# Eight rows of every down projection as seven-product groups, and the convolution's taps placed after a PSUM copy

## The reference

```python
def swiglu(x, w_gate, w_up, w_down):              # D_FF = 2816, two in each of two layers
    return (jax.nn.silu(x @ w_gate) * (x @ w_up)) @ w_down
...
up = h @ w_up[l]                                  # D_FF_2 = 3072, once, in the third layer
gate_h = causal_dwconv(up[..., :D_FF_2], ffn_conv_w[l], ffn_conv_b[l])   # three taps over positions
hid = jax.nn.gelu(gate_h) * up[..., D_FF_2:]
x = x + rms_norm(hid @ w_down[l], g_ffn_post[l])
```

## Time and profile before

| | us |
|---|---|
| median of 3 runs | 2766.65 |
| the three runs | 2766.55 to 2767.83 |
| the profiled execution: its own time | 2767.5 |
| its span, first to last instruction | 2765.7 |

### The profile page before, as it was taken

One profiled execution on the slowest core, in us unless ns is written; L12 is line 12 of the kernel. 1 busy time (PEld: TensorE's weight loads), 2 busy tenths in 40 slices (PEclk: granted clock), 3 DMA queues, 4 the chain that ended last, 5 costly groups with the idle time before them and its releaser, 6 DMA issues.

```text
span 2765.7 us, 43073 instructions
## 1 busy us (share of the span) xinstructions
PE 2752.3 (100%) x17466; PEld 2456.1 (89%) x17466; DVE 1844.3 (67%) x2529; ACT 1496.5 (54%) x2334; POOL 117.1 (4%) x130
## 2 busy tenths in 40 slices
PE   9999999999999999999999999999999999999999
PEld 8998887599998899998976799988987889999888
DVE  7766466767773587773667587753876746888638
ACT  6554343565563585553536565543755536666435
POOL 0000000000000000000000000000001100000000
PEclk9999999999999999999999999999999999999999
DMA  7773324037752237753241257733233223776331
GB/s 216 176 184 111 114 58 97 18 104 192 187 142 99 89 91 203 177 143 100 77 101 41 90 141 183 180 100 107 77 98 91 90 85 106 186 183 151 122 115 61
DMA packets 146965, 337.79 MB, mean 122 GB/s; under 512 B 34256, under 2 KB 58192, under 8 KB 146768
## 3 DMA queue, kind: packets, MB, share of 16 engines
q1 hardware_dynamic: 133376, 286.79, 33.4%
q0 software_dynamic: 13248, 48.24, 10.4%
q10 hardware_dynamic: 144, 0.00, 0.0%
HBM read 330.79 MB, written 2.10 MB: 120 GB/s over the span
## 4 chain that ended last, share of the span: by engine, by line
PE 94%; DVE 4%; ACT 1%; issue 1%; DMA 0%; SPq 0%; DVEq 0%; ACTq 0%
PE banks L676 29%; PE banks L677 29%; PE banks L678 29%; DVE WL L551 1%; PE banks L1178 1%; PE banks L1200 1%; ACT WH L546 1%; PE banks L1237 1%; PE banks L1189 1%; DVE CG L2078 0%; PE banks L1241 0%; PE banks L1227 0%; PE banks L715 0%; PE banks L1331 0%; DVE C L2344 0%
## 5 line engine op out<-in xcount | busy, mean ns | idle before, releaser
L676 PE MATMUL banks<-HH,WH 128*128 128x256 f32 (+1 forms) x2764 | 879.6, 318 | 1.4 <-DVE WL L2119 0.9
L677 PE MATMUL banks<-HH,WL 128*128 128x256 f32 (+1 forms) x2764 | 874.8, 316 | 0.0
L678 PE MATMUL banks<-HL,WH 128*128 128x256 f32 (+1 forms) x2764 | 874.5, 316 | 0.0
L551 DVE TENSOR_TENSOR WL<-raw,WH 128x1024 fp32r<-128x1024 f32 (+2 forms) x407 | 489.9, 1206 | 509.5 <-ACT WH L546 508.7
L546 ACT ACTIVATE WH<-raw 128x1024 fp32r<-128x1024 f32 (+2 forms) x407 | 422.1, 1040 | 598.1 <-PE banks L678 338.2
L676 PEld LDWEIGHTS banks<-HH,WH 128*128 128x128 f32 x2764 | 526.6, 191 | 44.5 <-issue 6.9
L677 PEld LDWEIGHTS banks<-HH,WL 128*128 128x128 f32 x2764 | 526.8, 191 | 34.6 <-issue 1.0
L678 PEld LDWEIGHTS banks<-HL,WH 128*128 128x128 f32 x2764 | 526.7, 191 | 34.0
L676 PE MATMUL banks<-SH,WH 128*128 128x256 f32 x1472 | 417.2, 283 | 3.2 <-DVE WL L551 3.2
L677 PE MATMUL banks<-SH,WL 128*128 128x256 f32 x1472 | 416.5, 283 | 0.0
L678 PE MATMUL banks<-SL,WH 128*128 128x256 f32 x1472 | 416.5, 283 | 0.0
(11 more groups left out here) (312 smaller groups left out, 3105.7 us busy)
## 6 DMA issues: line engine op xcount, KB each, us to landing
raw<-in_w_down SPq DMA_DIRECT2D x112, 512.0 KB, 3.5
extra_raw<-in_w_quarters SPq DMA_DIRECT2D x96, 512.0 KB, 4.2
raw<-in_w_in SPq DMA_DIRECT2D x68, 512.0 KB, 3.7
raw<-in_w_quarters SPq DMA_DIRECT2D x60, 512.0 KB, 4.5
extra_raw<-in_w_quarters POOLq DMA_DIRECT2D x36, 512.0 KB, 7.3
extra_raw<-in_up_quarters SPq DMA_DIRECT2D x26, 512.0 KB, 4.2
spare_raw<-in_w_quarters SPq DMA_DIRECT2D x24, 512.0 KB, 5.0
raw<-in_w_quarters POOLq DMA_DIRECT2D x24, 512.0 KB, 6.9
```

Source lines behind the costliest of these rows:

```text
L551: e.tensor_tensor(WL[tile_of[u]][:, 0:n], raw[raw_of(u)][:, 0:n], WH[tile_of[u]][:, 0:n].bitcast(F32), ALU.subtract).then_inc(*low.done((u,)))
L676: e.matmul(o, wh, ah, start=start, stop=False, skip_group_check=skip)
L677: e.matmul(o, wl, ah, start=False, stop=False, skip_group_check=skip)
L678: return e.matmul(o, wh, al, start=False, stop=stop, skip_group_check=skip)
```

## The change

Three things change, in all five `ffn` stages.

1. Down rows 0 to 7 are no longer eight rows of 24 matmuls of 512 tokens. They become two more seven-product groups, numbered n and n+1 (n is `gated_groups(s)`, 11 or 12): weights in quarters made on the host (`down_quarters`), the hidden rows as the four input blocks, and four sums of hidden blocks (`row_sum`) in place of the summed inputs. Group n gives output blocks 0 to 3 and writes its results straight into PSUM banks 0 to 3, group n+1 gives blocks 4 to 7 into tile C, and two ACT copies (`seeds`) put these into banks 4 to 7. Down rows 8 and later accumulate onto these banks.
2. Hidden rows 0 to 7 and the four row sums, with their high and low parts, must be ready as group n runs, so the work on them is placed between the operations of groups n-2 to n.
3. In stage 9 the operations on a group's halves (taps, GELU, convolution) are put in another order: `p1` comes ahead of the second half's taps.

```diff
+DOWN_SEVEN = 8
+SUM_QUADRANTS = ((0, 1), (0, 0), (1, 0), (1, 1))
 def seven_groups(s):
-    return range(2, (FF2 if s > 8 else FF) // 256)
+    return range(2, gated_groups(s) + 2)
...
+        for g in seven_groups(s)[-2:]:
+            for ph in range(PHASES):
+                self.add((s, "seven", g, ph))
-        for k in range(width // P):
+        for k in range(DOWN_SEVEN, width // P):
             self.add((s, "down", k), self.rows(down, l, k * P, 1, 0, D))
...
+        def seven_banks(s, g):
+            i = g - gated_groups(s)
+            return (7, 5, 6) if i == 0 else (4, 5, 6) if i == 1 else tuple(group_banks(g)[:3])
...
             def chunk(j, t):
+                if down:
+                    return lambda kp: (HIDH_HIGH[:, 2 * kp + j, part(t)], HIDL_LOW[:, 2 * kp + j, part(t)])
...
                     for kp in range(4):
+                        if down and ph in (0, 3) and up == 0:
+                            e.wait_ge(*vec.at("hidden_low", s, 2 * kp + (ph == 3)))
...
+            tensor_last_rows(e, s, [W[s, "down", k] for k in range(DOWN_SEVEN, 2 * n_groups)],
...
+                             [[first[b // 2]] if b < 4 else [act.at("seeds", s, b // 2 - 2)] for b in range(DC)],
+                             opens=False)
...
+        def scalar_row_sum_high(e, s, i):
+            e.wait_ge(*vec.at("row_sum", s, i))
+            e.activation(row_sums(HH, i), row_sums(HLF, i), ACT.Copy).then_inc(*act.done(("row_sum_high", s, i)))
+        def scalar_seeds(e, s, m):
+            n = gated_groups(s)
+            if m:
+                e.wait_ge(*vec.at("c12", s, n + 1))
+                e.wait_ge(*act.at("c21", s, n))
+            else:
+                e.wait_ge(*act.at("c21", s, n + 1))
+            e.activation(banks[:, 4 + 2 * m:6 + 2 * m, :], C[:, :, m, :], ACT.Copy).then_inc(*act.done(("seeds", s, m)))
...
         def vector_hidden_low(e, s, k):
             e.wait_ge(*act.at("hidden_high", s, k))
+            if k < DOWN_SEVEN:
+                e.wait_ge(*vec.at("row_sum", s, 2 + k % 2))
...
+        def vector_row_sum(e, s, i):
+            def rows(t, j):
+                return HIDF[:, j:DOWN_SEVEN:2, part(t)]
+            n = gated_groups(s)
+            one, other, op = ((rows(1, 0), rows(1, 1), ALU.subtract),
+                              (row_sums(HLF, 0), rows(0, 0), ALU.subtract),
+                              (rows(0, 0), rows(1, 0), ALU.subtract),
+                              (rows(0, 1), row_sums(HLF, 1), ALU.add))[i]
...
+        def vector_row_sum_low(e, s, i):
+            e.wait_ge(*act.at("row_sum_high", s, i))
+            e.tensor_tensor(row_sums(HL, i), row_sums(HLF, i), row_sums(HH, i).bitcast(F32), ALU.subtract).then_inc(
+                *vec.done(("row_sum_low", s, i)))
```

More of the change, by code:

```diff
@@ L470, in quadrant, with quarter_out @@
             return C[:, :, j, part(t)]
+        def quarter_out(s, g, t, m):
+            return banks[:, 2 * m:2 * m + 2, part(t)] if g == gated_groups(s) else quadrant(t, m)
         def pair(tile, m, h):
@@ L939, in tensor_ffn @@
         def tensor_ffn(e, s):
-            n_groups = groups(s)
+            n_groups = gated_groups(s)
             def cols(i, j):
@@ L1553, in after_seven @@
         def after_seven(s, g, i):
-            return W[s, "seven", g + 1, i] if g < seven_groups(s)[-1] else W[s, "down", i]
+            return W[s, "seven", g + 1, i] if g < seven_groups(s)[-1] else W[s, "down", DOWN_SEVEN + i]
         def scalar_full(e, s, *chunks):
@@ L1690, in scalar_ffn @@
+                scalar_copy(e, s, g, "u2", 2, x, quadrant(0, 1), *u2_free)
                 split_high(e, W[s, "seven", g, 6])
-                scalar_copy(e, s, g, "c11", 3, y, quadrant(0, 0), *((vec.at("hidden", s, 3),) if first else (
-                    vec.at("hidden_half", s, g - 1, 0), first_half_read(s, g - 1))))
+                if g > n:
+                    scalar_hidden_high(e, s, 10)
+                    scalar_hidden_high(e, s, 11)
+                scalar_copy(e, s, g, "c11", 3, y, quarter_out(s, g, 0, 0), *rest)
@@ L1715, in scalar_ffn @@
-            rows = 2 * groups(s)
-            for k in range(3, rows):
+                    scalar_row_sum_high(e, s, 1)
+                    scalar_hidden_high(e, s, 2)
+                if g > n:
+                    scalar_hidden_high(e, s, 12)
+                    scalar_hidden_high(e, s, 13)
+                scalar_copy(e, s, g, "u3", 4, x, quadrant(1, 1), *u3_free)
+                split_high(e, after_seven(s, g, 1))
+                if g == n - 1:
+                    scalar_hidden_high(e, s, 4)
+                    scalar_row_sum_high(e, s, 2)
@@ new lines, in scalar_ffn @@
+                if g > n:
+                    scalar_hidden_high(e, s, 14)
+                    scalar_hidden_high(e, s, 15)
+                split_high(e, after_seven(s, g, 2))
+                if g == n - 1:
+                    scalar_hidden_high(e, s, 6)
+                if g < n and not conv:
+                    scalar_silu_half(e, s, g, 0)
+            scalar_seeds(e, s, 1)
+            scalar_c21(e, s, n + 1)
+            scalar_seeds(e, s, 0)
+            for k in range(DOWN_SEVEN + 3, 2 * n):
@@ L1717, in scalar_ffn @@
                 split_high(e, W[s, "down", k])
-                for n in range(2 * k - 3, min(2 * k - 1, rows)):
-                    scalar_hidden_high(e, s, n)
-                if s == 0 and k == 10:
+                for row in range(2 * k - 6, min(2 * k - 4, 2 * n)):
+                    scalar_hidden_high(e, s, row)
+                if s == 0 and k == 14:
                     scalar_tables(e)
@@ L2460, in vector_ffn @@
                 split_low(e, W[s, "down", k])
-                for n in range(2 * k - 3, min(2 * k - 1, rows)):
-                    vector_hidden_low(e, s, n)
-                if s == 0 and k == 10:
+                for row in range(2 * k - 6, min(2 * k - 4, 2 * n)):
+                    vector_hidden_low(e, s, row)
+                if s == 0 and k == 14:
                     vector_tables(e)
```

267 lines of the change are left out of this document (165 added, 102 removed).

## The result

The changed kernel takes 2784.35 us (median of 4 runs, 2783.24 to 2785.07), the kernel before 2766.86 beside it (2766.55 to 2767.83): ratio 1.0062, 95% interval 1.0050 to 1.0075, 17.5 us slower. The profiled execution took 2784.8 us with a span of 2783.0. The forecast was +6.9 us and a range of 2762 to 2784. (The profile names PE's steps by the lines of the changed kernel now: L693 to L695 are the three matmuls of a trio, L2440 is `vector_hidden_low`, L568 the weights' low part.)

What follows compares the result with a forecast made beforehand. PE bounds the kernel, busy 2752.3 of 2765.7 us at full clock. Four SiLU stages at +1.5 us (+6.0) and stage 9 at +0.9 gave +6.9, so 2773.5 us for the median; range 2762 to 2784.

Steps and rivals of the forecast that it cites:

- What it removes on PE: Eight down rows (43.53 us) replaced by two seven-product groups (40.32): 3.21 us less per stage, 16.0 in all five.
- The taps: Stage 9: `p1` ahead of GELU and the second taps removes nine PE waits at the third product, 5.2 us.
- The 1.1 us of the first down row: Stage 9: the wait for the copy `c21` in the first down row goes with that row, 1.1 us.
- DVE's queue and the stall: SiLU stages, group 11's phase 0: DVE late for hidden rows 4 and 6, PE waits 4.6 us in two parts.
- less late: Rival, chance 0.22: DVE's waits for ACT close, each stall is 3.1 us, stage 9's 7; 2764 us.
- in time: Rival, chance 0.10: HIDL_LOW row 6 is written before PE wants it and no `u3` is late; 2744 us.
- The seeds: Start of down row 8: ACT's `seeds` for banks 4 and 5 end late for bank 4, 0.13 us taken.
- more is late: Rival, chance 0.12: seeds wait for a load or POOL's accumulated quarters come late, one microsecond a stage; 2779 us.
- Stage 9: Added waits of 10.4 us in stage 9, where the convolution makes DVE later; +0.9 us net with the savings.
- the clock falls: Rival, chance 0.10: PE's stalls bring half clock, 2.88 us in each of five stages, 14 more; 2788 us.
- the last of its signs of being wrong: Forecast wrong if hidden row 6's gap is under 3 or over 6 us, stage 0's `u3` late, or clock below full.

Runs made afterwards that it cites:

- fill_both: Changed kernel with 9 extra, never-read PE products ahead of each of the two waits in the first down group's phase 0, all five stages; 2776.26 us, ratio 1.0036.
- taps_only: Kernel before with only the changed order of taps, GELU and convolution halves in stage 9; 2761.0 us, ratio 0.9978.
- reordered: Changed kernel with its work around the first down group in another order, such as hidden rows 4 and 6 earlier on DVE; 2773.97 us, ratio 1.0026.
- no_sums: dve_sums with the first down group's two weight sums cut from 1024 to 8 columns, so not computing the reference; 2764.06 us, ratio 0.9988.
- dve_sums: reordered with row sum 3 and sum 1's low part ahead of the scaling, last HIDF product behind phase 5's low part; 2774.59 us, ratio 1.0027.
- fill_second: Changed kernel with 9 extra PE products ahead of the second wait (hidden row 6) alone; 2778.03 us, ratio 1.0038.
- pool_sums: dve_sums with the two weight sums of the first down group made on POOL instead of DVE; 2782.35 us, ratio 1.0055.
- early_sum: Changed kernel with only row sum 0 and its high part made two groups earlier; 2783.58 us, ratio 1.0060.

## Why the prediction was wrong

- **What it removes on PE**, 3.21 us a stage. No run shows it by itself. It fits: in fill_both stage 0 has -3.21 + 4.31 (the time that the gaps take) + 0.3 (in the down rows) = +1.4, and +1.63 is measured. The reason given beside it is off: by 0.1200 and 0.2267 a half-width matmul costs 0.0067 us more than half of a full one, not 0.013 (that is the excess of two). The sum does not use it.
- **The taps**, 5.2 us: right, 5.3 in the trace of taps_only. The 1.1 us of the first down row no run shows by itself; taps_only still has that row, and its 6.1 us hold 0.35 of it.
- **DVE's queue and the stall**, 4.6 us: right in place, form and cause, 4.3 measured, in two parts around three matmuls. The rivals *less late* and *in time* are out.
- **The seeds**, 0.13 a stage: too little in stage 9, where bank 4's first matmuls come 1.2 us late; 0.1 to 0.7 in the others. 2.5 us in all, 1.9 more than forecast. That is as much as came of *more is late*, which had one microsecond in every stage.
- **Stage 9**, 10.4 us of waits: `u2` 0.3 and `u3` 2.4 as forecast (0.4 and 2.5); rows 4 and 6 2.3 (forecast 4.0), phase 3 1.2 (1.6), phases 4 and 5 0.4 (0.5), phase 6 1.3 (1.3). A little too much, since PE itself came later.
- **The step that failed** is that the sum has a stall cost its length and no more: the half clock behind it stood at nothing. The sum of the forecast gave +6.9, and with the clock held up by extra products the kernel is at +9.2 (2776.26 to 2767.06); the seeds are 1.9 of the difference and the half clock left in stage 9 about 1.4, with hidden rows that were less late against them. Of the further 8.1 us some 7.3 are the clock. The prediction had it as the rival *the clock falls*, with the right place and mechanism, priced at 14 and given 0.10; the last of its signs of being wrong, a granted clock below full behind a gap, is the one that came. Its price was about 1.6 times too high (7.3, and 1.4 more in stage 9), since it took a whole phase's time for each of five stages; its chance was far too low. The argument against it was only that no row of before had such a wait. But that is exactly the situation in which the rows of before cannot speak for a full clock: it had no wait much above 1 us. A forecast that puts PE to near idleness for 4.6 us five times should have carried the half clock in its sum.

What kept the change from paying is in part shown and in part open. DVE is full in group 11 (6.80 of 6.80 us in the stretches above). Its order matters: reordered leaves +1.0 to +1.5 us per SiLU stage of the +3.1 to +4.0. Its load matters: with 2.3 us of its work left out the kernel is just under the one before (no_sums), but not under taps_only. And ACT's order matters, by the rows and not by a run of its own: in dve_sums and no_sums it is `p1`, behind a SiLU that waits for DVE, that holds the third product. Whether an order of both engines pays with all the work in place was not tried, nor was a layout with sums made elsewhere than on DVE and POOL.

## What to carry to other kernels

A wait on PE of two microseconds or more may not be priced by its length alone: read the granted clock of the stretch behind it, and where the trace of before has no such wait, put the half clock into the sum as a likely term, not as a rare case. Taking products off PE by sums made on another engine pays only if that engine has the time at the place where the first product wants its operand; an average of 67% said nothing about group 11, and moving a pass out ahead of a place where the engine waits for another only lengthens that wait. When a wait is called `issue` or a reordering changes nothing, look up what ended just before it: here the wait of the same place had passed from DVE to ACT. Split a change into its parts before judging it: here one part gave 6 us and the other took 23.

## What the runs showed of the hardware

The clock after a gap was not the same each time in the same place. Counted over the PE gaps of one profiled execution each:

```
gaps on PE (us beyond the usual start-to-start)          clock fell
1.2 to 1.9, alone (reordered, no_sums, others)           in no case seen
2.4 to 2.9, alone (fill_second 6, dve_sums 6, one each
  in stage 9 of the six other kernels with the groups)   9 of 18
3.3 to 3.4, alone (pool_sums)                            3 of 5
2.4 and 1.6 to 1.9 with three matmuls between
  (changed kernel 4, early_sum 4)                        8 of 8
```

Each time it stayed at half for 3.4 or 6.8 us. One more microsecond at half clock cost about 0.4 us (7.3 us for 20.4 in the SiLU stages, 1.4 for 3.4 in stage 9), less than half. Matmuls of 256 columns started 0.213 us apart there against 0.120, which is less than twice, and in part of the time PE was still waiting (1.9 of 6.8 us in stage 0).

In pool_sums an add of 128x1024 on POOL took 2.69 us, or 3.92 where DVE's passes went ahead, and a pass of DVE that began beside it could be held up until it was done: 2.83 us instead of 1.22, and 2.86 instead of 0.68.
